# Where a value product, three operands and a memset stand in the queues of a two-block attention and recurrence kernel

## The reference

```
first block:   h = rmsnorm(x);  q_a,k_a,v_a,g_a, q_b,k_b,v_b,g_b = split(h @ w_in)
               o_a = softmax(q_a k_a^T / 8) v_a * silu(g_a)                 # 8 heads, 2 key heads
               o_b = softmax(q_b k_b^T / 8 + bias, 8x16 neighbourhood) v_b * silu(g_b)   # 8 heads
               x = rmsnorm(x + concat(o_a, o_b) @ w_out)
second block:  proj = rmsnorm(x) @ w_in_2
               recurrence (8 heads of 64, state S of 64x64), for each token t:
                  S = S * w_t - (S kk_t)(kk_t a_t)^T + v_t k_t^T ;   y_t = S r_t
                  y = groupnorm(y) + sum(r * k * r_k) * v ;  y_a = (y * silu(z)) @ w_out_a
               latent causal attention -> y_b
               out = x + rmsnorm((gate_a * y_a + gate_b * y_b) @ w_o)
```

## Time and profile before

| | us |
|---|---|
| median of 3 runs | 1800.71 (1799.89 to 1800.97) |
| the profiled execution | 1800.97 |
| its span, first to last instruction | 1799.2 |
| TensorE busy | 1764.1 |
| VectorE busy | 933.7 |
| ScalarE busy | 798.4 |
| GpSimd busy | 449.6 |

### The profile page before, as it was taken

How to read it: one execution, slowest core, us unless ns; L and a number is a source line. 1 busy time by engine, 2 the same in 40 slices (tenths; PEclk the granted TensorE clock), 3 DMA queues, 4 the chain that set the end, 5 groups by cost and what they waited for, 6 DMA issues and landing times.

```text
span 1799.2 us, 39002 instructions
## 1 busy us (share of the span) xinstructions
PE 1764.1 (98%) x16429; PEld 1423.2 (79%) x16429; DVE 933.7 (52%) x2008; ACT 798.4 (44%) x1766; POOL 449.6 (25%) x459
## 2 busy tenths in 40 slices
PE   9999999999999999999999999999999999999998
PEld 8997766788888688977777777777777886668887
DVE  5667766423533626116555556555553267765513
ACT  5346666434534525224434344344343356655421
POOL 5640000012111533114324233333233201002221
PEclk9999999999999999999999999999999999999999
DMA  5143320233243252342222122123213320005432
GB/s 198 37 156 117 85 57 1 84 105 110 91 121 108 65 177 97 86 126 91 64 64 77 55 73 71 59 76 100 64 58 104 100 68 13 1 1 211 160 133 94
DMA packets 146006, 159.93 MB, mean 89 GB/s; under 512 B 15092, under 2 KB 123960, under 8 KB 145832
## 3 DMA queue, kind: packets, MB, share of 16 engines
q1 hardware_dynamic: 145800, 157.37, 27.4%
q0 software_dynamic: 32, 0.07, 0.0%
HBM read 110.53 MB, written 52.62 MB: 91 GB/s over the span
## 4 chain that ended last, share of the span: by engine, by line
PE 91%; DVE 3%; ACT 3%; issue 1%; DMA 1%; POOL 1%; SPq 0%; DVEq 0%; POOLq 0%; ACTq 0%
PE ps L1005 9%; PE ps L1007 7%; PE ps L1006 7%; PE ps L701 7%; PE ps L702 7%; PE ps L703 7%; PE ps L816 4%; PE ps L1134 4%; PE ps L795 3%; PE ps L895 3%; PE ps L897 3%; PE ps L896 3%; PE ps L803 3%; PE ps L1324 3%; PE ps L1347 2%; PE ps L1334 2%
## 5 line engine op out<-in xcount | busy, mean ns | idle before, releaser
L2863 POOL TENSOR_TENSOR t<-t,t 128x512 fp32r<-128x512 f32 x183 | 239.6, 1323 | 772.2 <-ACT t L1451 742.5
L1005 PE MATMUL ps<-t,t 128*128 128x512 f32 (+2 forms) x720 | 289.6, 402 | 1.4 <-POOL t L2863 1.4
L701 PE MATMUL ps<-t,t 128*128 128x256 f32 (+2 forms) x872 | 282.1, 324 | 1.7 <-ACT t L1458 1.0
L703 PE MATMUL ps<-t,t 128*128 128x256 f32 (+2 forms) x872 | 276.8, 317 | 0.0
L702 PE MATMUL ps<-t,t 128*128 128x256 f32 (+2 forms) x872 | 276.7, 317 | 0.0
L1007 PE MATMUL ps<-t,t 128*128 128x512 f32 (+2 forms) x720 | 268.9, 373 | 0.0
L1006 PE MATMUL ps<-t,t 128*128 128x512 f32 (+2 forms) x720 | 268.4, 373 | 0.0
L701 PEld LDWEIGHTS ps<-t,t 128*128 128x128 f32 x872 | 165.9, 190 | 15.0 <-issue 3.6
L703 PEld LDWEIGHTS ps<-t,t 128*128 128x128 f32 x872 | 165.9, 190 | 10.4
L702 PEld LDWEIGHTS ps<-t,t 128*128 128x128 f32 x872 | 166.1, 191 | 10.1 <-issue 0.4
L1005 PEld LDWEIGHTS ps<-t,t 128*128 128x128 f32 x720 | 136.2, 189 | 35.0 <-issue 12.8
(11 more groups left out here) (271 smaller groups left out, 3223.3 us busy)
## 6 DMA issues: line engine op xcount, KB each, us to landing
t<-in_w_in SPq DMA_DIRECT2D x53, 512.0 KB, 6.0
zgate_spill<-t SPq DMA_DIRECT2D x20, 512.0 KB, 2.9
tile_bias<-t SPq DMA_DIRECT2D x16, 576.0 KB
t<-tile_bias SPq DMA_DIRECT2D x8, 1152.0 KB, 6.0
t<-zgate_spill SPq DMA_DIRECT2D x16, 512.0 KB, 4.0
feat_spill<-t SPq DMA_DIRECT2D x13, 512.0 KB, 3.3
tile_bias<-band_bias SPq DMA_DIRECT2D x48, 128.0 KB
t<-values_and_gates SPq DMA_DIRECT2D x96, 64.0 KB
```

The costliest lines, as they stand in the source:

```text
L701: e.matmul(dst, lh, rh, start=k == 0, stop=False)
L703: m = e.matmul(dst, ll, rh, start=False, stop=k == n - 1)
L1005: e.matmul(dst, lh, rh, start=k == 0, stop=False)
L2863: e.tensor_tensor(WLO[wslot(b)][:, o], WST[:, o], WHI[wslot(b)][:, o].bitcast(F), ALU.subtract).then_inc(w_lo.sem, w_lo.up((b, p)))
```

## The change

It has three parts.

1. In the loop over the tiles of the neighbourhood attention, for p < 3, `band_value(m - 2)` moves: on TensorE from ahead of `band_scores(m)` to behind `band_turn(m - 1)`, on ScalarE from ahead of `band_turned(m - 1)` to behind it. For p = 3 it stood there before. On VectorE `band_output` takes the tile m - 3 rather than m - 2 in these rounds, and the QK part that follows has three outputs rather than two.
2. In a unit's program on VectorE one `yield STAGE_US` moves from behind `kh` to behind `b0`. The operations `bo`, `bh` and `kh` come out of step 6 and into step 7.
3. On GpSimd the memset of the state moves from step 10 to the start of the chain, behind the wait for the unit before.

```diff
@@ pe_program, neighbourhood attention
                     m = B_Z + 8 * p + n
-                    if p < 3 and n > 1:
-                        band_value(m - 2)
                     band_scores(m)
...
                     if n:
                         band_turn(m - 1)
-                    if p == 3 and n > 1:
+                    if n > 1:
                         band_value(m - 2)
                     if p < 3:
                         values_and_gates(p + 1, n, hi, lo, (7,))
@@ dve_program
                 for x, (what, half) in enumerate(QK):
-                    if p and x < 2:
-                        band_output(B_Z + 8 * p - 2 + x)
+                    if p and x < 3:
+                        band_output(B_Z + 8 * p - 3 + x)
                         if x == 0:
                             band_gates(B_Z + 8 * p - 1)
...
-                    if p < 3 and n > 1:
-                        band_output(m - 2)
-                    elif p == 3 and n > 2:
+                    if n > 2:
                         band_output(m - 3)
@@ dve_program, unit
                 e.tensor_tensor(BK[:, :, 0, :], ch3(TM[:, :]), ch3(E3[:, :]), ALU.mult).then_inc(*did("b0"))
+                yield STAGE_US
                 w.wait_ge(*prep_v[u, "b0"])
                 e.scalar_tensor_tensor(out=TM[:, :], in0=r_, scalar=vec("r_k", j), in1=k_, op0=ALU.mult, op1=ALU.mult).then_inc(*did("bo"))
                 e.tensor_tensor(ch3(CU[:, :]), BK[:, :, 0, :], bc(PCT[:, :], 2, 64), ALU.mult).then_inc(*did("bh"))
                 e.tensor_tensor(ch3(SG[:, :]), BK[:, :, 1, :], bc(PCT[:, :], 2, 64), ALU.mult).then_inc(*did("kh"))
-                yield STAGE_US
                 w.wait_ge(*prep_mm[u, "bonus"])
@@ pool_program, unit
                 plus_one(S.FT, NDT, "e4")
-                if h == 0:
-                    if u:
-                        w.wait_ge(*chain_mm[u - 1, "y", CU_ - 2])
-                    e.memset(S2[:, 0, :], 0.0).then_inc(*did("state"))
                 yield GRAM_US
...
                 while il.units < u:
                     yield 0
+                if h == 0:
+                    if u:
+                        w.wait_ge(*chain_mm[u - 1, "y", CU_ - 2])
+                    e.memset(S2[:, 0, :], 0.0).then_inc(*did("state"))
                 for c in range(CU_):
```

## The result

The changed kernel takes 1817.34 us (1816.79 to 1818.21), the kernel before 1800.3 (1799.32 to 1800.97), each the median of four runs. The ratio is 1.0096, 95% interval 1.0078 to 1.0113. That is 17.0 us more, where 1819.3 us in all (+18.3 on the profiled execution) was forecast. The profiled execution took 1818.21 us over a span of 1816.4.

A forecast was written before the change was run, and what follows sets the result against it. TensorE, busy 98% of the span, was taken as the bound. 1800.97 + 3.4 (part 1) + 9.6 (part 2) + 3.6 (part 3) + 1.7 (clock) = 1819.3 us; range 1808 to 1828, own case 1813 to 1824.

The forecast's parts named there:

- Part 1, +3.4 forecast: Attention pair stages, p = 0 to 2: a fourth tile-shape change makes 18 rounds 5.51 us, not 5.32; +3.4 us.
- The lower bound of 0: Part 1's lower bound: 0 us if waits, not tile shapes, make the holes; its bounds were 0 to +7.
- What VectorE and ScalarE do: Attention rounds: later exponentials on ScalarE and later outputs on VectorE were taken as hidden, at 0 us.
- Part 2, +9.6: Bonus product in odd units: TensorE stops, six times 1.27 and two times 1.0 us; bounds 7 and 18.
- The even units: Part 2 in even units: one small VectorE operation comes between, hidden, 0 us; unit 4 the tightest.
- Part 3, +3.6: Chain start: TensorE waits for the memset behind a weight split, 1.8 us each in units 0 and 12; bounds 0 and 7.
- The clock, +1.7: TensorE's granted clock: one more drop to the lower level after the new stops, +1.7 us; bounds 0 and 8.5.
- one in four stops: Clock term: one of four long TensorE stops in the profile of before was followed by a drop costing 1.7 us.
- GpSimd did not hold the moved operations: Rival, odd units: GpSimd's split holds the moved VectorE operations, each stop grows by 1.0 us; 1827.3 us, chance 0.12.
- the lower clock grew by one stretch and not by four: Rival on the clock: it falls behind every second of ten stops, five drops of 1.7 us; 1826.1 us, chance 0.12.
- nothing hid the stops: Rival on part 2: later TensorE waits shrink by the earlier stops, leaving 1 us; total 1809, chance 0.11.
- moving the memset did not help the spread: Rival on part 3: GpSimd reaches the spread's pow and copy earlier, 4.0 us of waits vanish; 1795, chance 0.03.

The follow-up runs named there:

- e2_yield: Kernel before with only part 2, the moved VectorE yield: 1810.05 us against 1800.3, ratio 1.0051, +9.8 us.
- e7_spread_early: Kernel before with GpSimd's pow and copy for the kk spread one step earlier in its program: 1795.5 us against 1800.18, ratio 0.9977.
- e8_even_yield: Kernel before with the yield of part 2 moved in the even units alone: 1800.51 us against 1800.18, ratio 0.9998.
- e5_bo_back: Kernel before with only `bh` and `kh` put behind the yield, `bo` staying ahead: 1807.01 us against 1800.18, ratio 1.004.
- e1_band: Kernel before with only part 1, the moves in the neighbourhood attention: 1803.48 us against 1800.3, ratio 1.0016, +3.2 us.
- e3: Kernel before with only part 3, the moved GpSimd memset: 1804.14 us against 1800.3, ratio 1.002, +3.8 us.
- e6: Part 3 on the kernel before, but with the memset one step earlier, at the end of step 16: 1800.59 us against 1800.18, ratio 1.0002.
- e9: Kernel before with TensorE order turn, value, scores, dense, ScalarE as in part 1, VectorE's order kept: 1802.33 us against 1800.1, rounds of 5.36 us.
- e4: The first of those experiments: kernel before with TensorE order turn, value, scores, dense, and part 1's VectorE and ScalarE orders: 1815.07 us, ratio 1.008.

## Why the prediction was right

**Part 1, +3.4 forecast.** The stretch lost 3.72, of which the rounds are 3.4, and alone the part costs 3.2. The crossings read off elsewhere in the same trace gave 5.51 us a round, and 5.51 it is. That the shape of the tile is the cause was argued; the other order of the round bears it out, with 5.36 us for three changes. What each change costs by itself, 0.1 to 0.2 in the prediction, isn't measured. The lower bound of 0 is out. The Trainium skill (TensorEngine Tiling (Array Packing), Key Properties) names a drain at each change of the tiling mode, without a price. No row shows a drain as such, but the rounds agree with it: the fourth change costs 0.15 us (5.51 against 5.36). What VectorE and ScalarE do was costed at nothing. In the rounds that was right; in the QK part of p = 3 it came to the 0.3 us above. And the first of those experiments shows how thin that was: with the value product 0.9 us earlier and the output where part 1 has it, 13 us came of it.

**Part 2, +9.6.** The six stops of 1.27 us are 1.27 us to the start of the product, and 1.34 to the turn behind it. Units 5 and 11 lose 0.87 rather than 1.0, since the first of the copies follows the held operation by 1.41 us from its start (984.93 to 986.34), where the bonus input had followed it by 1.52. That makes 6 x 1.34 + 2 x 0.87 = 9.8, and part 2 alone measures +9.8. The even units cost nothing, as forecast. But the tightest of them is unit 0 and not unit 4, as the wait of 0.27 in unit 0 shows; the lower clock at 818 hid that in the profile of before.

**Part 3, +3.6.** Two stops of 1.67, not 1.8: the memset starts 0.06 us before the split's record ends, and the split took 1.26. Alone +3.8.

**The clock, +1.7.** This term was mis-sized: it came to 0.1. The lower clock lasts longer by one stretch, but the part that was added at p = 3 cost only the 0.14 us of the table above, where TensorE also waits for ScalarE and VectorE (the waits of L871 fell from 3.1 to 1.9 us). The stretch that vanished at 818 gave back 1.6: the two timelines are 3.53 us apart at the last scores and 1.95 at the turn just ahead of unit 0's product (825.04 and 826.99). That product then lost 0.4 again, as it caught VectorE too early. The stretch behind unit 5 cost 1.6. So 0.14 - 1.6 + 1.6 = 0.1. Against the 18.3 forecast for the span, 17.2 is then 1.6 less for the clock, 0.3 less at the start of the kernel and 0.25 less in part 3, and about 1.0 more from part 1, part 2 and unit 0.

That the lower clock lasted longer by just one stretch is luck. The count of one in four stops was drawn from a single profile, and where the lower clock falls changes from one profile to the next without a change in the stops. The stretch at p = 3 is long in seven of the eleven profiles and short in four (before, e2_yield, e7_spread_early, e8_even_yield). The stop of unit 0's spread, 1.41 to 1.42 us in ten profiles, has one behind it in the profile of before alone.

The rivals: GpSimd did not hold the moved operations (the bonus input took 0.47 to 0.48 us in all eight odd units; the 1.37 to 1.40 of three even units was there before too, and hides), the lower clock grew by one stretch and not by four, nothing hid the stops, and moving the memset did not help the spread.

## What to carry to other kernels

Where one engine is busy all the time, read its queue from start to start and not from its waits: a change of tile shape and the first 0.16 us of a stop stand in no list. The price of a new order can be put together from crossings that the old trace already has elsewhere. A small operation that a busy engine waits for belongs ahead of the long one of its queue, with its operands' true time in mind: part 3 lost 3.8 us by the wrong side of a 1.28 us split, and the same rule applied to the spread won 4.7.

## What the runs showed of the hardware

A fourth change of TensorE's tile shape in a round cost 0.15 to 0.19 us in steady rounds without any wait: 5.32 or 5.36 us a round with three changes, 5.51 with four.

The lower clock followed a stop of 1.41 us (before, until 816.78) and of 2.26 us (unit 5, after and in e2_yield), and two close together of 1.39 and 0.57 (unit 5 in e5_bo_back). It did not follow one of 1.7 (before, until 1031) or 1.6 (after, unit 0's chain). The same stop had it in some profiles and not in others: behind the 1.41 to 1.42 us of unit 0's spread there was one in one profile of ten, and behind the 1.65 to 1.68 us of unit 6's spread there was one in six of them (e1_band, with 0.57 over 1034 to 1038, and e2, e3, e6, e8 and e9), and none in those of before, after, e4 and e5. Which stops are followed by one, these runs don't settle. Where TensorE waits for others anyway, 3.4 us more at half the clock cost 0.14; in the dense products behind unit 5 as long a stretch cost 1.6.
